# A one-core two-block kernel: the first attention's heads computed by token, the squares' sum ahead of chunk 4, later asks for c and the context

## The reference

```python
# q, k: 4 heads of 128; v: 4 heads of 256; i, f: gates, one per head and direction
hc_f, s_f = mlstm_chunk_scan(qc, kc, vc, ic[0], fc[0], s0, emit_ctx)      # context first
hl_f, _ = mlstm_chunk_scan(ql, kl, vl, il[0], fl[0], s_f, True)           # then the tokens
# (the same backwards gives hl_b)
    num = jnp.einsum('bhts,bhsv->bhtv', w, vc) + ...
    den = jnp.sum(w, axis=-1) + ...
    h = num / jnp.maximum(jnp.abs(den), jnp.exp(-m_t))[..., None]
y = mlstm_readout(hl_f + rq(hl_b), ol, head_gain, w_out)
    hn = h * lax.rsqrt(jnp.mean(h * h, axis=-1, keepdims=True) + EPS)     # per head, over its 256
    y = (hn * gain * jax.nn.sigmoid(o)) @ w_out
```

## Time and profile before

| | |
|---|---|
| median of three runs | 1456.73 us |
| profiled execution: its own time / its span | 1456.49 / 1454.7 us |
| busy share of the span: PE, PEld, DVE, ACT | 95%, 81%, 79%, 54% |
| chain that ended last: PE, DVE, ACT, DMA, issue | 80%, 10%, 5%, 3%, 2% |
| DMA engines, mean busy share, 0 to 20 and 20 to 40 us | 0.90 and 1.00 |
| first output projection begins | 239.0 us |

### The profile page before, as it was taken

One profiled execution on the slowest core, in us unless ns is written; L12 is line 12 of the kernel. 1 busy time (PEld: TensorE's weight loads), 2 busy tenths in 40 slices (PEclk: granted clock), 3 DMA queues, 4 the chain that ended last, 5 costly groups with the idle time before them and its releaser, 6 DMA issues.

```text
span 1454.7 us, 19174 instructions
## 1 busy us (share of the span) xinstructions
PE 1382.9 (95%) x7530; PEld 1183.9 (81%) x7530; DVE 1146.6 (79%) x1629; ACT 784.0 (54%) x1114; POOL 1.4 (0%) x6
## 2 busy tenths in 40 slices
PE   6999988899998999999999999999999999999998
PEld 4888966788886888879887888878888888788886
DVE  5786688799977988878777988779889777887653
ACT  6613443666635555456356655376554555665542
...
GB/s 384 214 244 249 147 49 130 219 254 234 258 340 138 327 289 293 319 233 229 251 129 187 306 277 287 335 192 302 286 287 304 269 154 60 202 280 198 187 189 58
DMA packets 62715, 337.79 MB, mean 232 GB/s; under 512 B 6929, under 2 KB 9361, under 8 KB 34209
## 3 DMA queue, kind: packets, MB, share of 16 engines
...
## 4 chain that ended last, share of the span: by engine, by line
PE 80%; DVE 10%; ACT 5%; DMA 3%; issue 2%; SPq 0%; DVEq 0%; ACTq 0%
PE bank L253 77%; DVE wlo L249 2%; DMA raw<-w_stream 2%; ACT rstd L543 1%; ACT whi L242 1%; DVE mring L755 1%; ACT T L597 1%; DVE rd L1420 1%; PE bank L514 1%; DVE T L607 1%; DMA mring<-m_stream 1%; DVE SGC L672 1%; DVE X L685 1%; DVE EF L1422 0%; PE bank L730 0%
## 5 line engine op out<-in xcount | busy, mean ns | idle before, releaser
L253 PE MATMUL bank<-hh,whi 128*128 128x512 f32 (+1 forms) x2192 | 675.0, 368 | 8.3 <-DVE wlo L249 8.1
L249 DVE TENSOR_TENSOR wlo<-raw,whi 128x2048 fp32r<-128x2048 f32 x219 | 500.6, 2288 | 71.1 <-ACT whi L242 71.0
L253 PE MATMUL bank<-hh,wlo 128*128 128x256 f32 x1896 | 533.1, 281 | 0.0
L242 ACT ACTIVATE whi<-raw 128x2048 fp32r<-128x2048 f32 x219 | 418.4, 1915 | 163.6 <-PE bank L253 109.9
L253 PEld LDWEIGHTS bank<-hh,whi 128*128 128x128 f32 x2192 | 395.5, 190 | 85.0 <-DVE wlo L249 8.0
L253 PEld LDWEIGHTS bank<-hh,wlo 128*128 128x128 f32 x1896 | 360.5, 190 | 0.0
L253 PE MATMUL bank<-whi,hid_hi 128*128 128x512 f32 x440 | 172.2, 391 | 0.0
L253 PE MATMUL bank<-whi,hid_lo 128*128 128x512 f32 x440 | 171.3, 389 | 0.0
L253 PE MATMUL bank<-wlo,hid_hi 128*128 128x512 f32 x440 | 171.2, 389 | 0.0
L253 PE MATMUL bank<-whi,hh 128*128 128x512 f32 x480 | 158.4, 400 | 1.6 <-DVE hh L622 0.8
L755 DVE SCALAR_TENSOR_TENSOR mring<-mring,con 128x1024 f32<-128x1024 f32 x107 | 130.6, 1220 | 18.8 <-DMA mring<-m_stream 18.7
...
## 6 DMA issues: line engine op xcount, KB each, us to landing
raw<-w_stream SPq DMA_DIRECT2D x219, 1024.0 KB, 5.0
...
```

The costliest lines, as they stand in the source:

```text
L242: nc.scalar.activation(w_hi(c, 0, CW), raw[:, c % RAW_SLOTS], ACT.Copy).then_inc(s_hi, 1)
L249: nc.vector.tensor_tensor(w_lo(c, 0, CW), raw[:, c % RAW_SLOTS], w_hi(c, 0, CW).bitcast(f32), ALU.subtract).then_inc(s_lo, 1)
L253: return nc.tensor.matmul(out, lhsT, rhs, start=start, stop=True, skip_group_check=True)
```

## The change

Three things are changed.

**The heads go by token.** `EF` becomes the stationary operand, one tile of 128 keys by 128 tokens, and V the moving one: `head_rows(h, t)` gives for a half t of the tokens and each direction 128 tokens by 257 columns, of which the last is the denominator, because V gets a column of ones for every head. Tiles that a direction's mask empties are left out, so that a head has 14 matmuls of 257 columns. Thresholds are turned into columns once (two small transposes), `invert` works on 128x2, `first_direction` (ACT) and `directions` (DVE) scale and add the two directions, `rows_rstd` (ACT) makes the norm of each row, `normalise` (DVE) applies it, `turn_head` turns the head back with four transposes, `gated` applies gain and gate. Gone are `denominators`, `magnitudes`, `numerators`, the squares' sums in the heads and the threshold half of `rows`. The engines' orders in the heads are written anew.

**First stage.** The squares' sum of x stands ahead of chunk 4. The context is asked for after chunk 9 in place of chunk 7; GpSimd asks for the row `c` when DVE has split chunk 8 in place of chunk 2, and ACT's silu of it moves from between chunks 5 and 6 to behind the copies of x, with a table load ahead of it and one behind.

**Units.** The four units that stood ahead of chunk 12 on DVE are now done in the heads.

```diff
     for k in range(DT):
+        if k == 4:
+            pe.wait_ge(s_in[6], 16)
+            pe_stat(pe, N_X1)
         pe.wait_ge(s_lo, k + 1)
         for g in range(4):
             mm(bank[g][:], c4[:, k], w_hi(k, g * 512, (g + 1) * 512), k == 0)
             ins = mm(bank[g][:], c4[:, k], w_lo(k, g * 512, (g + 1) * 512), False)
         ins.then_inc(s_pe, 1)
-        if k == 4:
-            pe.wait_ge(s_in[1], 32)
-            pe_stat(pe, N_X1)
...
-            mm(bank[2 + d][:, 0:SEQ], cst("sel")[0:36, q:q + P], mt[:], True)
-            ins = mm(bank[2 + d][:, SEQ:], cst("sel")[0:36, q:q + P], th[:], True)
+            ins = mm(bank[2][:, d * SEQ:(d + 1) * SEQ], cst("sel")[0:36, q:q + P], mt[:], True)
...
     scores(0)
     output_gate(0)
     rows(1)
     output_gate(1)
     scores(1)
+    pe.wait_ge(s_vb, 8)
+    head_rows(0, 0)
+    head_rows(0, 1)
     output_gate(2)
+    rows(2)
     scores(2)
+    head_rows(1, 0)
+    head_rows(1, 1)
+    rows(3)
     output_gate(3)
+    scores(3)
+    head_rows(2, 0)
+    head_rows(2, 1)
     pe.wait_ge(s_os, 4)
+    turn_head(0)
+    head_rows(3, 0)
+    turn_head(1)
+    head_rows(3, 1)
+    turn_head(2)
+    out_chunk(0)
+    turn_head(3)
+    out_chunk(1)
+    pe.wait_ge(s_y1, 2 * HEADS)
     pe_gate_row(pe, "lstm", (5, 6))
     pe_out_last(pe, c + 15, 4, hhi, hlo, HEAD_TAIL, lambda: out_chunk(2), lambda: out_chunk(3))
...
-    act.wait_ge(s_in[4], 16)
-    nc.scalar.activation(cb[:], cb[:], ACT.Silu).then_inc(s_cb, 1)
...
+    act.wait_ge(s_in[4], 16)
+    nc.scalar.activation(cb[:], cb[:], ACT.Silu).then_inc(s_cb, 1)
+    act.preload_act_table_set(LN_EXP)
...
-    dve.wait_ge(s_cb, 1)
-    mods(dve, 4)
...
     weighted(0)
     mods(dve, 1)
     exponents(1)
+    mods(dve, 1)
+    weighted(1)
+    invert(0, 0)
+    directions(0, 0)
+    invert(0, 1)
+    directions(0, 1)
     dve_split(dve, c + 12)
+    normalise(0, 0)
+    normalise(0, 1)
     mods(dve, 1)
+    exponents(2)
+    mods(dve, 1)
+    weighted(2)
+    invert(1, 0)
+    directions(1, 0)
+    invert(1, 1)
+    directions(1, 1)
+    exponents(3)
+    normalise(1, 0)
+    normalise(1, 1)
+    dve_split(dve, c + 13)
+    mods(dve, 1)
+    weighted(3)
+    invert(2, 0)
+    mods(dve, 1)
+    directions(2, 0)
+    invert(2, 1)
+    directions(2, 1)
+    gated(0)
+    invert(3, 0)
+    rest_head(0)
+    gated(1)
+    normalise(2, 0)
+    normalise(2, 1)
+    directions(3, 0)
+    invert(3, 1)
+    gated(2)
+    directions(3, 1)
+    rest_head(1)
+    dve_split(dve, c + 14)
+    normalise(3, 0)
+    normalise(3, 1)
+    rest_head(2)
+    mods(dve, 3)
+    dve_split(dve, c + 15)
+    mods(dve, 1)
+    gated(HEADS - 1)
     dve_mod_bias(dve, 24, 40)
     dve_pre_coef(dve, "f0")
+    rest_head(HEADS - 1)
+    dve_split(dve, c + 16)
+    dve_split(dve, c + 17)
     dve_split(dve, c + 18)
...
-    chunks(6, 8)
+    chunks(6, 10)
     sp.dma_start(XC[:], ctxT).then_inc(s_in[2], 16)
-    chunks(8, 12)
+    chunks(10, 12)
     sp.dma_start(con[:, 2 * P:], const_d[:, 2 * P:]).then_inc(s_in[5], 16)
...
-    pool.wait_ge(s_lo, 3)
+    pool.wait_ge(s_lo, C_LSTM + 1)
     pool.dma_start(cb[:], c_row.partition_broadcast(P)).then_inc(s_in[4], 16)
```

More of the change, by code:

```diff
@@ L331, in tok, with pe_out_chunk @@
             return buf[:, k, t * P:(t + 1) * P]
-        def pe_out_chunk(pe, c, k0, hi, lo, first):
+        def pe_out_chunk(pe, c, k0, hi, lo, first, fourth=None):
             for g in range(2):
                 for t, h in GROUPS:
+                    if fourth is not None and (t, h, g) == (1, 1, 0):
+                        pe.wait_ge(*fourth)
                     ins = mm3w(out_bank(t, h), c, g * D + h * 512, tok(hi, k0 + g, t), tok(lo, k0 + g, t),
@@ L751, in dve_mod_unit @@
             dve.wait_ge(s_mod[unit_slot(u)], 16 * unit_loads(u))
-            if u == COND_UNITS:
-                dve.wait_ge(s_cb, 2)
+            if u in (0, COND_UNITS):
+                dve.wait_ge(s_cb, 2 if u else 1)
             a = FIRST_MODS + u
@@ L1016, in build, with row_bank, turned_bank @@
         s_uT, s_uc = sem("u_columns"), sem("u_columns_read")
-        s_os, s_ad, s_sg = sem("o_bank_read"), sem("denominators_abs"), sem("o_sigmoid")
+        s_os, s_sg = sem("o_bank_read"), sem("o_sigmoid")
         s_s = sem("qk_scores")
         s_arg, s_e = sem("decay_exponents"), sem("decay_weights")
-        s_p, s_den = sem("weighted_scores"), sem("denominators")
-        s_th, s_gw2, s_num = sem("threshold_read"), sem("normalised_scores"), sem("numerators")
+        s_p, s_num, s_rc = sem("weighted_scores"), sem("head_rows"), sem("denominators_inverted")
+        s_y0, s_y1, s_yr = sem("first_direction_scaled"), sem("directions_added"), sem("head_rows_rstd")
+        s_yn, s_yt = sem("head_rows_normalised"), sem("head_rows_turned")
         s_y = sem("gated_tile")
         EXPS = 6
-        def head_bank(h):
-            return bank[(6, 4)[h % 2]]
+        def row_bank(t, d):
+            return bank[4 + 2 * t + d]
+        def turned_bank(h):
+            return bank[3 if h < HEADS - 1 else 4]
         def pe_lstm(pe):
@@ L1143, in pe_lstm @@
                                           ident[0:36, 0:36])
+            for t in range(2):
+                ins = nc.tensor.transpose(bank[1][:, (4 + t) * 36:(5 + t) * 36], th[:, t * P:(t + 1) * P],
+                                          ident[0:36, 0:36])
             ins.then_inc(s_uT, 1)
@@ L1211, in values_read @@
                 for b in (1, 3):
-                    nc.scalar.activation(V[:, b, half * 512:(half + 1) * 512], bank[b + 4 * half][:], ACT.Copy)\
+                    nc.scalar.activation(V[:, b, 2 * half:2 * half + 2, 0:DV],
+                                         bank[b + 4 * half][:].rearrange("p (h v) -> p h v", h=2), ACT.Copy)\
                         .then_inc(s_vb, 1)
@@ L1272, in act_lstm @@
             decay(1, 0)
+            act_split(act, c + 12)
             gate_read(1)
-            magnitudes(0)
-            gate_read(2)
-            magnitudes(1)
+            first_direction(0, 0)
+            first_direction(0, 1)
+            rows_rstd(0, 0)
+            rows_rstd(0, 1)
+            act_split(act, c + 13)
+            gate_read(2)
+            decay(2, 1)
+            decay(2, 0)
+            act_split(act, c + 14)
+            first_direction(1, 0)
+            first_direction(1, 1)
+            rows_rstd(1, 0)
+            rows_rstd(1, 1)
+            act_split(act, c + 15)
+            decay(3, 1)
+            decay(3, 0)
             gate_read(3)
```

168 lines of the change are left out of this document (48 added, 120 removed).

## The result

| | before | after |
|---|---|---|
| runs on the same chip | 1457.47 us median, 4 runs | 1437.87 us median, 4 runs (1433.15 to 1441.24) |
| ratio | | 0.9866, 95% interval 0.9833 to 0.9900 |
| profiled execution: its own time / its span | 1456.49 / 1454.7 us | 1439.11 / 1437.3 us |
| busy: PE, DVE, ACT | 95%, 79%, 54% | 95%, 78%, 55% |

The change makes the kernel 1.34% faster. 1439.0 was forecast.

What follows compares the result with a forecast made beforehand. TensorE, busy nearly the whole span, bounds the kernel. First stage -2.7, chunk 12 -4.8, heads' work -8.0 and waits -2.2 make -17.7 us on 1456.49, giving 1438.8; forecast 1439.0, range 1430 to 1448.

Steps and rivals of the forecast that it cites:

- first stage: Start of the kernel: `mrow` copied at 35.2 us in place of 37.82, through earlier sum and later loads; -2.7 us.
- chunk 12: PE's standstill at 76.8 us and the half clock behind it go, less a new wait for the keys' copy; -4.8 us.
- heads, busy time of PE: Heads: less matmul work -8.0 us, less time at half clock -3.3, fewer drains and restarts at waits -0.8.
- heads, waits of PE up to the gate row: Heads ahead of the last projection: old waits go, a new one of 8.8 us comes; -3.1 us.
- last projection and x's rows: Behind the heads: new waits ahead of the last projection and at x's first turning, with half clock; +5.0 us.
- behind 240 us: Rest of the kernel after the heads: nothing changes behind the first boundary; 0 us.
- The keys' copy: Behind chunk 12: PE waits 0.6 to 0.7 us for the first keys' copy, which ends at 83.2 us.
- the rival of a second pass: The 56 `head_rows` matmuls: 257 columns cost 0.87 us each, 24.4 us more, 1463 us; chance 0.04.
- The wait of 8.8 us: PE's head 3 waits for DVE work queued behind head 1's `normalise`, which waits for head 0's turning; 8.8 us.
- the wait at head 3's turning: Turning of head 3: PE waits because `normalise` stands behind a chunk on DVE; 0.7 us.
- three terms: Waits of 2.0 us ahead of the last projection and 1.4 at x's first turning, and 1.6 of half clock.
- taking back: First feed-forward: if the weight stream bounds it, PE waits longer there and the lead is lost; 1450 us, chance 0.05.

Runs made afterwards that it cites:

- start_only: The kernel before with only the changed first stage; the four units stay ahead of chunk 12 and the heads are old: 1454.2 us, ratio 0.997.
- units_back: The changed kernel with the four units again ahead of chunk 12 and four fewer in the heads: 1439.63 us, 0.9872 of before.
- turn_early: As `normalise_late`, and PE also turns head 0 between the two halves of head 2's rows: 1425.39 us, 0.9771 of before.
- units_spread: As `turn_early`, with one of the three units ahead of chunk 23 done earlier, ahead of head 3's weighted scores: 1424.27 us, 0.9765 of before.
- sum_back: The changed kernel with the squares' sum behind chunk 4 again: 1439.69 us, 0.9867 of before.
- normalise_late: The changed kernel with DVE doing chunk 21, two units and head 3's weighted scores ahead of head 1's `normalise`: 1426.98 us, 0.9782 of before.

## Why the prediction was right, point by point

By its own steps, in the profiled execution (the table's parts):

| step | forecast | measured |
|---|---|---|
| first stage | -2.7 | -1.4 (A); in the seven kernels with the same start and the new heads -1.4 to -3.1, mean -2.2 |
| chunk 12 | -4.8 | -4.6 (B) |
| heads, busy time of PE | -8.0 - 3.3 (clock) - 0.8 | -13.4 |
| heads, waits of PE up to the gate row | -3.1 | -3.8 |
| last projection and x's rows | +5.0 | +4.9 (D) |
| behind 240 us | 0 | +0.9 (E), less than E's own spread |
| sum | -17.7 | -17.4 |

**First stage: right in its place; the 1.3 us missing behind it are the clock's.** All that was said of `mrow` came to pass, and PE left the wait 2.8 us earlier. The sum put nothing for what follows: TensorE comes out of its 3.3 us of wait at half clock, and how long that lasts differs between profiles of the same code. Eight kernels that are the same up to A (`start_only` is the eighth) leave the wait between 36.73 and 37.09 and are at A between 52.79 and 54.54. They fall in two groups: in three the granted clock over the next 12 us was 0.86, as before (39.87 to 55.91), and A is 2.8 to 3.1 us earlier than before; in five it was 0.72 or 0.73, and A is 1.4 to 1.8 us earlier. So the term was right for an equal clock, and its shortfall in the changed kernel is bad luck. Why the clock came back late in five isn't shown.

**Chunk 12: right, and it is the join of two edits.** -5.3 in its place by `units_back`, less the 0.6 us by which B is longer there than before: with the units in place the silu's later place holds them up. The keys' copy cost 0.98 us, not 0.6 to 0.7.

**Heads.** `head_rows` costs (202.72 - 199.68) / 7 = 0.434 us a matmul, forecast 0.433, so the rival of a second pass is out. The wait of 8.8 us was 8.51, and of what I had listed behind `normalise`. The half clock behind it took 2.0 us, forecast 2.7; the wait at head 3's turning 0.21, forecast 0.7. PE's busy time fell by 13.4 us, of which the clock is 6.0 - 2.0 = 4.0; the other 9.4 are 0.6 more than the 8.0 + 0.8 worked out. The transposes are half of that: four have a pitch of 0.44 us (182.06 - 181.62 in `turn_early`), so 16 cost 1.8 us and not 2.1. The rest stays open. `start_only` against `units_back` gives -14.4 us for the heads' code with four units fewer; the units add 2.0: -12.4, for a forecast of -8.0 - 2.2 = -10.2. The heads gave 2 us more than forecast, the first stage 1.3 less in this profile: that the sum came within 0.3 us is in part luck.

**Last projection: the right sum, with one term that isn't one.** D was forecast within 0.1 us from three terms: 2.0 us ahead of chunk 23 (1.84 measured), 1.4 at x's rows (1.22), 1.6 of half clock. That the third unit's row (2.46 us late) is behind the first is shown by `units_spread`. That chunks 24 to 26 ahead of the update are behind the second is read from the order and from VectorE's row of three splits; no run moves them, and the wait of 1.71 us that stays in `units_spread` fits. The half clock is there (granted 0.83 in the 10 us from 217.87), but it costs nothing in D: in `sum_back`, whose heads are the same, the same 10 us ran at 1.00, and D is 25.37 against 25.41. At full clock PE waits longer there (0.80 us for chunk 24, 1.66 at x's rows), since VectorE, busy 9.93 of these 10 us in both, ends last.

**Downstream.** No taking back is seen beyond what E varies by: the lead of 18.3 us at 240 us is 17.4 at the end; `turn_early`, 29.4 us ahead there, ends 32.4 ahead, and `normalise_late`, 27.2 ahead, ends 24.7 ahead. The mean E of the nine kernels with the new heads is 1196.3, the two with the old ones have 1196.0 and 1192.5.
